# Sample attention issued between the first gate products of a hybrid decoder layer

## The reference, cut to what matters

```python
p = _split_in(jnp.einsum('btd,dn->btn', x, w_in))
...
o_fox = fox_fn(fq, fk, fv, logf).reshape(B, T, -1).astype(x.dtype)   # prompt: causal; sample: paged
...
ob = jnp.stack([o_gla, o_fox, o_conv], axis=2)
br = jnp.einsum('btjc,jcd->btjd', ob, w_branch)          # (512 -> 1024) for each of 3 branches
g = jax.nn.sigmoid(p['gate'].reshape(B, T, N_BRANCH, D_MODEL))
mix = jnp.einsum('btd,de->bte', jnp.sum(g * br, axis=2), w_out)
```

```python
k_past = jnp.take(k_pool, page_table, axis=0).reshape(DB, past, FOX_H, FOX_HD)
...
s = jnp.einsum('bqhd,bkhd->bhqk', q_blk, k) * (FOX_HD ** -0.5)
s = s + (jnp.swapaxes(cq_blk, 1, 2)[..., :, None] - ckT[..., None, :])
p = jax.nn.softmax(jnp.where(kpos[None, :] <= qpos[:, None], s, -jnp.inf), axis=-1)
return jnp.einsum('bhqk,bkhd->bqhd', p, v)
```

## Time and profile before

| what | us |
|---|---|
| median of 3 runs | 1867.82 (1865.41 to 1872.73) |
| the profiled execution | 1866.79 |
| span of the profiled execution | 1865.1 |
| busy PE, share of the span | 1661.6, 89% |
| busy DVE | 834.4, 45% |
| busy ACT | 650.1, 35% |
| busy POOL | 246.0, 13% |
| mean granted clock of PE | 0.924 of full speed |

### The profile page before, as it was taken

The page is one execution under the profiler, slowest core; times in us unless marked ns, Lnnn a source line. Parts: engine busy times, 40 slices in busy tenths (PEclk is TensorE's granted clock), DMA queues, the critical chain, the costliest instruction groups (busy, mean ns, idle before and its releaser), DMA issues. The chain is left out here.

```text
span 1865.1 us, 25855 instructions
## 1 busy us (share of the span) xinstructions
PE 1661.6 (89%) x9847; PEld 1522.3 (82%) x9847; DVE 834.4 (45%) x1341; ACT 650.1 (35%) x1076; POOL 246.0 (13%) x320
## 2 busy tenths in 40 slices
PE   7999999996999998698999999999899299999950
PEld 6988898896988887597999999999788278888840
DVE  3433453441033343120222322222363689999947
ACT  4422322112154453211111211111211188888852
POOL 1000120021011111213000000000000123333114
PEclk9999999998999998655999999999999599999985
DMA  5111131123302110242311321320231678988538
GB/s 167 37 35 47 59 118 35 44 89 102 95 26 73 35 45 19 70 158 82 121 35 35 130 68 34 130 68 1 103 113 57 209 237 277 325 308 308 193 124 254
DMA packets 155300, 208.33 MB, mean 112 GB/s; under 512 B 14835, under 2 KB 121347, under 8 KB 155176
## 3 DMA queue, kind: packets, MB, share of 16 engines
q1 hardware_dynamic: 132472, 130.86, 22.7%
q0 software_dynamic: 22704, 75.79, 12.0%
HBM read 161.78 MB, written 44.84 MB: 111 GB/s over the span
## 5 line engine op out<-in xcount | busy, mean ns | idle before, releaser
L1852 PE MATMUL ps<-xh,slab_hi 128*128 128x384 f32 (+1 forms) x576 | 189.2, 328 | 8.3 <-POOL gt_first L1813 5.9
L1852 PE MATMUL ps<-xl,slab_hi 128*128 128x384 f32 (+1 forms) x576 | 188.8, 328 | 0.0
L1852 PE MATMUL ps<-xh,slab_lo 128*128 128x384 f32 (+1 forms) x576 | 188.8, 328 | 0.0
L375 PE MATMUL ps<-xh,slab_hi 128*128 128x384 f32 (+1 forms) x504 | 173.2, 344 | 1.2 <-DVE xl L730 1.2
L1895 DVE TENSOR_TENSOR gt_sg<-ps,gt_sg 128x384 f32<-128x384 f32 (+1 forms) x72 | 38.6, 536 | 293.9 <-PE ps L1852 293.9
L375 PE MATMUL ps<-xl,slab_hi 128*128 128x384 f32 (+1 forms) x504 | 166.5, 330 | 0.0
L375 PE MATMUL ps<-xh,slab_lo 128*128 128x384 f32 (+1 forms) x504 | 166.4, 330 | 0.0
L1867 ACT ACTIVATE gt_sg<-ps 128x384 f32<-128x384 f32 (+1 forms) x72 | 34.0, 474 | 298.6 <-PE ps L1852 298.5
L1852 PEld LDWEIGHTS ps<-xh,slab_hi 128*128 128x128 f32 x576 | 109.0, 189 | 9.0 <-issue 7.5
L1852 PEld LDWEIGHTS ps<-xh,slab_lo 128*128 128x128 f32 x576 | 109.0, 189 | 0.0
L1852 PEld LDWEIGHTS ps<-xl,slab_hi 128*128 128x128 f32 x576 | 109.0, 189 | 0.0
(11 more groups left out here) (463 smaller groups left out, 3945.9 us busy)
## 6 DMA issues: line engine op xcount, KB each, us to landing
slab_raw<-in_w_in SPq DMA_DIRECT2D x60, 512.0 KB, 4.3
mo_raw_g<-in_w_e_gate SPq DMA_DIRECT2D x16, 1024.0 KB, 6.1
mo_raw_u<-in_w_e_up SPq DMA_DIRECT2D x16, 1024.0 KB, 9.0
mo_raw_d<-in_w_e_down SPq DMA_DIRECT2D x16, 1024.0 KB, 5.1
y_dram<-mo_y POOLq DMA_DIRECT2D x32, 512.0 KB, 4.2
gt_oh<-oT_hi SPq DMA_DIRECT2D x3, 2176.0 KB, 8.1
gt_ol<-oT_lo SPq DMA_DIRECT2D x3, 2176.0 KB, 13.1
slab_raw<-in_w_branch SPq DMA_DIRECT2D x24, 256.0 KB, 6.1
```

Of the source, the lines that this page charges most:

```text
L375: mm = eng.matmul(out, w[:, b, k, :], x[:, k, t0:t0 + tn], start=(k == 0 and j == 0), stop=(k == KC - 1 and j == 2), skip_group_check=True)
L1852: last = eng.matmul(out, w[:, s % 2, c, wk, :], x[:, k, t0:t0 + tn], start=(k == 0 and i == 0), stop=(k == ks[-1] and i == 2))
```

## The change

Sample attention loses its stage and becomes part of `stage_gates`. The 24 gate units of branch 0 are cut into 96 pieces (quarters of a unit, 6 matmuls each, two chunks of the contraction), and PE issues them between the parts of sample attention: 8 pieces first, one behind each page of keys (17), two between the small steps of the head pairs, and, in each of the four value products, one behind each of the first three quarters. The other 38 follow. After them come all branch products of j = 0, and then j = 1 and 2 as before, with the loops written out.

- The gate of j = 0 is written by ACT straight into `m`, and the branch product is multiplied in place; nothing is added for j = 0, and POOL no longer clears `m`.
- The weights of j = 0 are loaded in 8 parts: n = 0 to 3 for gates (8 chunks), n = 4 to 7 for branches (4 chunks), n = 8 to 15 whole. The first is loaded and split in `stage_fox`, at Q = 24 on ACT and on DVE (before: on ACT and on POOL, in the sample stage).
- The key ring has four buffers for six. These, the probabilities and the constants lie in the part of `m` that is written late, in `sg`, and in spare parts of the weight buffers; `ln1_g` is loaded into the place of the sample queries, keys and values.
- Gates of j = 0 use the PSUM banks 4 and 7, sample attention 0 to 3, 5 and 6.
- In the loop over j = 1 and 2, SP loads one weight pair ahead of the mixer outputs (before: two), so `head_gates` of the second pair of a branch stands, on ACT, before its first sigmoid and waits for a load issued after the mixer outputs'.

```diff
@@ stage_fox, SP, ACT, DVE
+            eng.wait_ge(w_tail, NBLK)
+            eng.wait_ge(p_tr, k_chunk[3, 2] + 1)
+            load_gates(sh, eng, 0)
...
+                if Q == 24:
+                    eng.wait_ge(unit_mm, kq_unit(3, 1, 2) + 1)
+                    head_gates(sh, eng, 0)
...
+                if Q == 24:
+                    tail_gates(sh, eng, 0)
@@ load_gates, head_gates
+    if n > 0:
+        eng.wait_ge(sh.g_split, n)
...
+    eng.wait_ge(sh.g_loaded, 32 * (n + 1) if n < 8 else 256 + 64 * (n - 7))
+    eng.activation(hi[:, n % 2, :, ks], raw[:, :, ks], ACT.Copy).then_inc(sh.g_head, 1)
@@ stage_gates, SP
+            for i in range(3):
+                load_page(i)
+            load_gates(sh, eng, 1)
+            for i in range(3, RK):
+                load_page(i)
...
+            load_gates(sh, eng, 2)
+            load_gates(sh, eng, 3)
+            eng.wait_ge(pv_mm, 4)
+            load_branch(0)
+            load_gates(sh, eng, 4)
...
+            for j in (1, 2):
+                eng.wait_ge(m_done, UJ * j)
+                load_branch(j)
+                for s in range(1, 5 if j == 1 else 4):
+                    load_gates(sh, eng, 4 * j + 4 + s)
@@ stage_gates, PE
+            def gate_piece(n):
+                u, part = divmod(n, 4)
+                s, c, g = u // 6, u % 6 // 3, u % 3
+                if part == 0:
+                    if u % 6 == 0:
+                        eng.wait_ge(split, s + 1)
+                    if u >= 2:
+                        eng.wait_ge(sg_ready, u - 1)
+                t0, tn = GROUPS[g]
+                out = sh.ps[:, gate_bank(0, u), 0:tn]
+                for k in (2 * part, 2 * part + 1):
+                    for i, (w, x) in enumerate(((w_hi, sh.xh), (w_hi, sh.xl), (w_lo, sh.xh))):
+                        mm = eng.matmul(out, w[:, s % 2, c, k, :], x[:, k, t0:t0 + tn], start=(k == 0 and i == 0),
+                                        stop=(k == KC - 1 and i == 2), skip_group_check=True)
+                if part == 3:
+                    mm.then_inc(gate_mm, 1)
...
+            def weigh_between(p, n):
+                for part in range(4):
+                    weigh_values(p, part)
+                    if part < 3:
+                        gate_piece(n + part)
...
+            gate_pieces(0, FIRST)
             for i in range(NP + 1):
                 if i < NP:
                     transpose_keys(i)
                 if i >= 1:
                     past_scores(i - 1)
+                gate_piece(FIRST + i)
             eng.wait_ge(pool_s, POOL_DONE)
             decay()
+            gate_pieces(25, 27)
             eng.wait_ge(c_in, 16)
             row_scores(0)
+            gate_pieces(27, 29)
             row_scores(1)
+            gate_pieces(29, 31)
             transpose_probs(0)
+            gate_pieces(31, 33)
             row_scores(2)
...
+            gate_pieces(58, 96)
+            for s in range(4):
+                eng.wait_ge(split, 4 + s + 1)
+                for c in range(2):
+                    branch(0, s, c)
@@ stage_gates, ACT
+            first_gate(0)
+            head_gates(sh, eng, 1)
+            first_gate(1)
+            for i in range(0, NP, 2):
+                place_keys(i)
+                if i % 4 == 2:
+                    first_gate(2 + i // 4)
+            exponent(0)
+            first_gate(6)
+            exponent(1)
+            place_probs(0)
+            first_gate(7)
+            exponent(2)
+            head_gates(sh, eng, 2)
+            first_gate(8)
...
+            for s in range(4):
+                eng.wait_ge(br_mm, 6 * s + 6)
+                head_gates(sh, eng, 6 + s)
@@ stage_gates, DVE
+            tail_gates(sh, eng, 1)
             for i in range(1, NP, 2):
...
+                place_keys(i)
```

More of the change, by code:

```diff
@@ new lines, in stage_gates @@
+        late = [sh.m[:, fb, :] for fb in range(8)]
+        after, ones, at = late[5][:, 0:128], late[5][:, 128:256], late[5][:, 256:384].rearrange("p (i h) -> p i h", h=H_FOX)
+        tsel, bsel = late[5][0:DT, 384:512], late[5][0:DB, 512:640]
+        tmask, bmask = late[5][0:DT, 640:704], late[5][0:DB, 704:768]
+        P = late[6][:, 0:2 * KN].rearrange("p (b n) -> p b n", b=2)
+        ST = late[7][:, 0:512].rearrange("p (b i h t) -> p b i h t", b=2, i=NP, h=2)
+        PTn = late[7][0:DB * DT, 512:768].rearrange("p (b n) -> p b n", b=2)
@@ L1537, in _, with load_page @@
         def _(eng):
-            for i in range(NP):
+            def load_page(i):
                 if i >= RK:
@@ L1612, in transpose_probs, with weigh_values @@
                 mm.then_inc(p_tr, 1)
-            def weigh_values(p):
+            def weigh_values(p, part):
                 cc = slice(128 * p, 128 * p + 128)
                 out = sh.ps[:, 1, cc]
[L1617 to L1622, removed]
+                if part == 0:
+                    if p == 0:
+                        eng.wait_ge(v_in, 16 * NP)
+                    eng.wait_ge(pn_out, p + 1)
+                    eng.wait_ge(pt_out, p + 1)
+                    eng.matmul(out, sh.vs[:, cc], PTn[:, p % 2, :], start=(p == 0), stop=False, skip_group_check=True)
+                for i in range(4 * part, 4 * part + 4):
@@ new lines, in units @@
+            def units(j, s, c, kind, bank, ks, hi, lo, done):
+                for g, (t0, tn) in enumerate(GROUPS):
+                    v = 3 * (2 * s + c) + g
+                    if v >= 4:
+                        eng.wait_ge(m_done, UJ * j + v - 3)
+                    elif j == 0 and v >= 2:
+                        eng.wait_ge(sg_ready, UJ - 3 + v)
+                    out = sh.ps[:, bank(v), 0:tn]
+                    for k in ks:
+                        wk = k + (8 if kind == "branch" else 0)
+                        for i, (w, x) in enumerate(((w_hi, hi), (w_hi, lo), (w_lo, hi))):
+                            last = eng.matmul(out, w[:, s % 2, c, wk, :], x[:, k, t0:t0 + tn],
+                                              start=(k == 0 and i == 0), stop=(k == ks[-1] and i == 2))
+                    last.then_inc(done, 1)
@@ L1628, in _, with gates, branch @@
+            def gates(j, s, c):
+                units(j, s, c, "gate", lambda v: gate_bank(j, v), range(8), sh.xh, sh.xl, gate_mm)
+            def branch(j, s, c):
+                if s == 0 and c == 0:
+                    eng.wait_ge(o_in, 32 * j + 32)
+                units(j, s, c, "branch", branch_bank, range(4), oh, ol, br_mm)
+            gate_pieces(0, FIRST)
             for i in range(NP + 1):
@@ L1862, in branch @@
+            tail_gates(sh, eng, 4)
+            tail_gates(sh, eng, 5)
+            for s in range(4):
+                for u in range(6):
+                    multiply(6 * s + u)
+                tail_gates(sh, eng, 6 + s)
+            for j in (1, 2):
                 for s in range(4):
                     for u in range(6):
-                        v = 6 * s + u
-                        t0, tn = GROUPS[u % 3]
-                        eng.wait_ge(gate_mm, UJ * j + v + 1)
-                        eng.activation(sg[:, v % 4, 0:tn], sh.ps[:, v % 4, 0:tn], ACT.Sigmoid).then_inc(sg_ready, 1)
@@ L1878, in _ @@
[L1878 to L1901 removed]
+                        accumulate(j, 6 * s + u)
```

406 lines of the change are left out of this document (199 added, 207 removed).

## The result

| | median us | runs |
|---|---|---|
| before | 1867.47 | 4, 1865.41 to 1872.73 |
| changed | 1822.13 | 4, 1820.67 to 1824.29 |

The ratio is 0.9761, 95% interval 0.9735 to 0.9787: 2.4% faster. The profiled execution of the changed kernel has a span of 1818.8 us for 1865.1. Predicted were 1820 us. Two later groups of runs of the same kernel gave 1825.97 (6 runs, 1819.09 to 1828.60) and 1823.29 (5 runs, 1817.32 to 1827.63); why they scatter by some 10 us is a part of what follows.

What follows compares the result with a forecast made beforehand. PE's own work was taken as the bound, with idle edges and half-clock sample work to win. Terms -96.7 - 6.1 + 43.6 + 4 + 3 + 2 + 3 = -47.2 us turn 1867.8 into 1820.6, said as 1820; range 1808 to 1840.

Steps and rivals of the forecast that it cites:

- first gate product earlier: Start of the merged stage: gate products begin at about 778.0 instead of 874.7, 96.7 us sooner.
- wait and low clock at j = 0: Start of branch products: PE's 4.40 us wait for mixer outputs and 1.7 us lost to lower clock go, -6.1 us.
- 386 small records: Sample attention's matmuls on PE: at full clock 0.113 us each, 43.6 us in all instead of 84.3.
- switches: First matmul of a piece behind small products costs about 0.1 us more, some 40 times: 4 us, bounds 2 and 6.
- wait for the first key copy: Start of merged stage: PE waits about 3 us for ACT's key copy, behind pair 1's head split; bounds 0 and 8.
- two boundaries j: At j = 1 and 2, PE waits for an accumulation delayed by the second pair's load: 2 us in all, 0 to 8.
- rival 1: Merged stage: clock stays at 1.2 GHz, PE pays double for 58 pieces and sample work; 108 us more, about 1925; chance 0.05.
- rival 2: Key pages: the clock falls there alone, 41 us more, 1861 us; chance 0.04.
- rival 4: Sample attention: small products cost the same at either clock, so its work stays 84 us, time 1861; chance 0.01.
- rival 3: Merged stage and j = 1, 2: start and j waits, late key ring or table loads take part; about 1838; chance 0.18.
- The prompt at Q = 24: Prompt attention: DVE's tail waits for ACT's head, delaying the normalisation and Q = 25's value products; 3 us, bounds 0 and 4.
- The rule on transposes: Key pages: full clock doesn't engage for transposes, so the pages' 64 transposes are the likeliest place to fall back.

Runs made afterwards that it cites:

- e1: Changed kernel with no gate pieces inside the sample attention: 8 before it, pieces 8 to 95 behind it; 1862.17 us, ratio 0.9985 to the kernel before.
- e2: Changed kernel with only the 17 gate pieces among the key pages moved behind the last page; 1839.85 us, ratio 0.9859 to the kernel before.
- e7: Changed kernel with only the tail split at Q = 24 moved from DVE to POOL; 1818.83 us, ratio 0.9732 to the kernel before.
- e8: Changed kernel with first key copies before pair 1's split, second weight pairs before mixer outputs (j = 1, 2), Q = 24 tail on POOL; 1811.87 us, ratio 0.9703.
- e5: Changed kernel with only ACT and DVE copying key pages 0 and 1 before they split pair 1; ratio 0.9739 to the kernel before, runs 1812.74 to 1823.05 us.
- e10: Changed kernel with unsplit value products, their three pieces behind each, and key pages 0 and 1 copied before pair 1's split; 1822.35 us, ratio 0.977.
- e9: Changed kernel with a piece behind every second key page, and key pages 0 and 1 copied before pair 1's split; ratio 0.9745, runs 1816.58 to 1829.68 us.
- e4: Changed kernel with each of the four value products unsplit, its three gate pieces behind it; 1830.88 us, ratio 0.9807 to the kernel before.
- e3: Changed kernel with a piece behind every second key page, the other nine behind the pages; runs 1819.20, 1821.86, 1847.51 and 1844.30 us, ratio 0.9849.

## Why the prediction was right, and where it was not

The bound was read rightly: 84 us of small products at half clock, and idle edges. e1 shares the gain out: of the 45 us, 41 depend on the pieces between the small products, and 4 are left when the edges alone are gone (e1's own small waits and clock rise are in that).

The time was near, and a part of that is luck. Against 1820 forecast, the three groups gave 1822.13, 1825.97 and 1823.29 us; by the ratios that is 1 to 6 us more than forecast. The first profile, which the table compares term by term, is the one of three without a fall of the clock at the start; the other two lost some 7 us in a term that the forecast did not have.

| step | predicted | measured in the first profile |
|---|---|---|
| first gate product earlier | -96.7, less 3 for the prompt's delay | -96.45, the delay included |
| wait and low clock at j = 0 | -6.1 | gone: no idle PE between 793 and 971 |
| 386 small records | 43.6, at 0.113 each | 42, at 0.109 |
| switches | 4 | 4 |
| wait for the first key copy | 3 | 2.8 |
| two boundaries j | 2 | 3.5 |
| end of the gate stage | -47.2 | -48.0 |

The 0.109 comes from the 84 us of 800 to 884: 601 records, 270 of them gate products (192 of 384 columns at 0.173 us and 78 of 320 at 0.147, together 44.7 us), and 36 switches at 0.09. (84 - 44.7 - 3.2) / 331 = 0.109. The switches of the whole stage are 42, 3.8 us. The terms measured, with the -6.1 as forecast, add up to -50.2, so 2.2 us of the stage are in no term; the span lost another 1.7 us behind it.

*The edges.* The 10.5 us between the blocks stayed, as forecast. Clock and pieces behaved as the prompt's rows had them. Rivals 1, 2 and 4 are answered by e1, e2 and the rows above: the clock is up with the pieces and at 0.50 without them; small products cost 0.22 us each at 0.50 (e1: 68.4 us for 313) and 0.109 at 1.00. (The time of rival 1 adds up to 1928, not 1925.) Of rival 3, the waits at the start and at j = 1 and 2 came, near their forecast sizes; the key ring and the 8 more table loads on ACT cost nothing here, as PE is busy 177.93 of the 178 us from 793 to 971. What rival 3 did not name either is the clock that falls with such a wait.

*The prompt at Q = 24.* The mechanism was right. Head and tail run one behind the other, and PE waits for the output that DVE normalises behind them, 3.03 us, and then 0.80 us more in the place of the 1.44 of the earlier trace rows:

```profile
716.32 2.29 DVE L1504 TENSOR_TENSOR slab_lo<-slab_raw,slab_hi 128x2048 fp32r<-128x2048 f32 x1 [2.16 <-ACT slab_hi L1497]
...
719.07 0.47 PE L1218 MATMUL ps<-ident,fx_o_tm 128*128 128x128 f32 x1 [3.03 <-DVE fx_o_tm L1433]
...
720.77 1.97 PE L1227 MATMUL ps<-fx_v,fx_PT 128*128 128x64 f32 x8 [0.80 <-DVE fx_ol L1438]
```

The value products of Q = 25 start 3.62 us later than in the earlier trace rows, and 0.66 us of that was there one step before (714.21 for 713.55): 3.0 us, as forecast. But the last product of the prompt came only 0.55 us later than before (767.41 for 766.86). The clock of its last steps was another: 0.50 at 720 to 730 and 0.95 at 740 to 750, where the kernel before had 0.67. Over all profiles of this kernel and of the experiments but e7 and e8, whose prompt part is the same, the next stage begins anywhere from 774.1 to 786.4 us. A single profile can't price 3 us there.

*The wait for the first key copy.* Predicted 3, measured 2.8, 2.7 and 2.6 us. What the prediction did not price is what comes with it: in two of three profiles of the changed kernel the clock then fell, for 6.8 us of loss each (stage 495.5 and 496.9 us for 491.1; the stages differ by less, since the first profile lost 3.9 us of clock behind the later waits and these two 1.4 and 2.0). Rows of the kernel before had shown such a thing, at j = 0, where 4.4 us of idle time were followed by a clock of 0.83; I charged it there as a saving and didn't ask the same of the new wait. With e5 and e8, which take the wait away, the clock is 1.00 through all of the sample attention and the stage 486.5 and 485.1 us. Over all experiments, 7 of the 9 profiles that have this wait (2.4 us or more) have a fall that begins in it or 0.2 us behind it, and none of the 4 without it (e5, e8, e10, and e9 with its 0.34 us) has one at this place. What sets the two apart that waited and did not fall is not shown: their waits, 2.78 and 2.76 us, are among the longer ones.

*The boundaries.* Predicted 2 us, measured 8.9 - 5.4 = 3.5. The fourth gate unit of j = 2 waits 2.2 us for an accumulation, as `head_gates` stands ahead of the sigmoids; at j = 1 it doesn't:

```profile
985.73 0.44 PE L1776 MATMUL ps<-gt_oh,slab_hi 128*128 128x384 f32 x1 [1.96 <-DMA gt_ol<-oT_lo]
...
1134.87 0.44 PE L1776 MATMUL ps<-gt_oh,slab_hi 128*128 128x384 f32 x1 [2.84 <-DMA gt_ol<-oT_lo]
1147.45 0.69 PE L1776 MATMUL ps<-xh,slab_hi 128*128 128x384 f32 x1 [2.23 <-DVE m L1973]
```

*The step that was wrong.* "Splitting the value products in four only spreads the pieces [...] It is worth about 0." It was sized from one run of small products at a full clock in the prompt, 3.61 us of values and 4.26 us to the next piece. e4 and e10 show runs of such a length (4.0 us where the clock held) with the clock falling inside or just behind them, in two of four in e4 and in three of four in e10: 6.8 us lost in e4's profile, 5.1 in e10's, and a stage 6.9 us longer in e10 than in e5. e4's stage is 4.4 us longer than the first profile's, which had the same wait and no fall of the clock there. So the split is worth some 4 to 7 us of the gain. It did not touch the forecast time, since that had the clock at 1.00.

*The rule on transposes* from the Trainium skill ("TensorE: Matmul & The Clock Gate", part 4) pointed at the pages as the likeliest place of a fall. The traces don't single out the pages: each fall there came in or right behind a wait of PE, and e5, e8 and e10, without a wait and with a piece behind every page, ran all 64 key transposes at 1.00. In e4 and e10 the clock fell, with no wait, in or just behind value products, which are no transposes.

What stays open: whether bare pages would bring the clock down without a wait (e2 with e5's edit was not run); whether e9's clock fell by its two short waits or by the order of the products; why the prompt's last steps take either clock, and with them some 10 us of scatter; why e7 gained more than its wait; and the size of e5's gain in runs.

The version that beats both kernels is e8: 1811.87 us, 3.0% under the kernel before and 0.7% under the changed one.

## What to carry to other kernels

Small products on TensorE can run at half clock though the engine never stops; laying them between large ones from an independent stage gave 41 of 45 us here, where removing the idle edges alone gave 4. How finely they are mixed matters: with a piece behind every page a fallen clock was back after 14 to 17 us, with none it stayed at 0.50 until the pieces came, and with one behind every second page both a quick return (6 us) and a slow one (30 us) were seen. Price a new wait near such a mix with the clock that may fall in it (some 7 us here for a wait of 2.7), and time and profile a version several times, because one profile in three of the same kernel had no fall.

## What the runs showed of the hardware that I had not expected

One program with no change between runs gave 1819 and 1847 us (e3), with mean clocks over the run of 0.949 and 0.931: the granted clock can differ between executions of one program. The profiles of the changed kernel show it in the mixed stretch itself: an idle PE of 2.7 us came with a fall of the clock in one execution and not in another (0.59 and 1.00 over 790 to 800). The number of columns did not set the cost of the small products: at a clock of 1.00, 32 records of 16 columns took 3.60 us in e4 (870.05 to 873.65), 0.113 us each, as much as the prompt's 64 columns; in runs of eight among the key pages they took 0.101 us each (802.14 to 802.95).
